# Attention over heads of 64: keys without zero halves, two heads' score products on the two row halves, units in pairs

## The reference, cut to what matters

```python
# first block, per query block
s = jnp.einsum('bqhd,bqjd->bhqj', qb, k_sel).astype(jnp.float32) * scale
p = jax.nn.softmax(jnp.where(valid[:, None], s, neg), axis=-1).astype(v.dtype)
return jnp.einsum('bhqj,bqjd->bqhd', p, v_sel)
```

## Time and profile before

| | us |
|---|---|
| median of 3 runs | 3588.89 (3577.92 to 3591.3) |
| profiled execution, its time | 3573.0 |
| its span, first to last instruction | 3571.1 |
| PE busy | 3265.0 |
| DVE busy | 1950.1 |
| ACT busy | 1306.1 |
| POOL busy | 490.5 |

### The profile page before, as it was taken

How to read it: one execution, slowest core, us unless ns; L and a number is a source line. 1 busy time by engine, 2 the same in 40 slices (tenths; PEclk the granted TensorE clock), 3 DMA queues, 4 the chain that set the end, 5 groups by cost and what they waited for, 6 DMA issues and landing times. The chain is left out here.

```text
span 3571.1 us, 45008 instructions
## 1 busy us (share of the span) xinstructions
PE 3265.0 (91%) x17008; PEld 2733.1 (77%) x17008; DVE 1950.1 (55%) x3638; ACT 1306.1 (37%) x2723; POOL 490.5 (14%) x410
## 2 busy tenths in 40 slices
PE   8998999999989999599979899999798979799996
PEld 6877788878777888488758778888687669688885
DVE  4776434347764343365765456564474864565654
ACT  4454423234544232242542233234342632332324
POOL 1031000010310000003026301010030128001010
PEclk9999999999999999798989999999897989899998
DMA  4111222131112221222000122221321000123231
GB/s 157 62 37 48 85 102 97 48 118 51 48 48 83 95 95 60 90 99 71 1 1 1 36 81 94 98 94 59 110 90 36 1 1 1 57 92 103 88 104 47
DMA packets 37327, 240.04 MB, mean 67 GB/s; under 512 B 4464, under 2 KB 5232, under 8 KB 14960
## 3 DMA queue, kind: packets, MB, share of 16 engines
q1 hardware_dynamic: 36528, 234.96, 19.2%
q10 hardware_dynamic: 576, 2.10, 0.2%
HBM read 234.95 MB, written 2.10 MB: 66 GB/s over the span
## 5 line engine op out<-in xcount | busy, mean ns | idle before, releaser
L259 PE MATMUL ps<-b_hl,bff_whl 128*128 128x512 f32 x704 | 275.4, 391 | 2.8 <-DVE b_hl L618 2.8
L261 PE MATMUL ps<-b_hl,bff_whl 128*128 128x512 f32 x704 | 274.8, 390 | 0.0
L260 PE MATMUL ps<-b_hl,bff_whl 128*128 128x512 f32 x704 | 274.8, 390 | 0.0
L242 DVE SCALAR_TENSOR_TENSOR bff_whl<-ring,b_cols,bff_whl 128x512 fp32r<-128x512 f32 (+1 forms) x224 | 153.2, 745 | 201.7 <-ACT bff_whl L229 201.5
L239 DVE TENSOR_TENSOR aff_whl<-ring,aff_whl 128x512 fp32r<-128x512 f32 x160 | 99.9, 686 | 224.0 <-ACT aff_whl L227 223.9
L259 PE MATMUL ps<-a_hl,aff_whl 128*128 128x512 f32 x512 | 201.3, 393 | 2.8 <-DVE a_hl L618 2.8
L229 ACT ACTIVATE bff_whl<-ring,b_cols 128x512 fp32r<-128x512 f32 (+1 forms) x224 | 136.6, 681 | 180.7 <-PE ps L261 180.7
L259 PE MATMUL ps<-aff_whl,a_u 128*128 128x512 f32 x512 | 202.0, 395 | 0.0
L261 PE MATMUL ps<-aff_whl,a_u 128*128 128x512 f32 x512 | 202.0, 395 | 0.0
L260 PE MATMUL ps<-aff_whl,a_u 128*128 128x512 f32 x512 | 202.0, 395 | 0.0
L260 PE MATMUL ps<-a_hl,aff_whl 128*128 128x512 f32 x512 | 200.9, 392 | 0.0
(11 more groups left out here) (493 smaller groups left out, 8093.2 us busy)
## 6 DMA issues: line engine op xcount, KB each, us to landing
ring<-in_a_w_ff SPq DMA_DIRECT2D x64, 1024.0 KB, 4.7
ring<-in_b_w_up SPq DMA_DIRECT2D x32, 1024.0 KB, 4.9
ring<-in_a_w_in SPq DMA_DIRECT2D x16, 1024.0 KB, 5.4
ring<-in_b_w_down SPq DMA_DIRECT2D x16, 1024.0 KB, 4.8
ring<-in_b_w_in_att SPq DMA_DIRECT2D x12, 1024.0 KB, 4.8
ring<-in_b_w_up SPq DMA_DIRECT2D x16, 768.0 KB, 4.2
ring<-in_b_w_in_conv SPq DMA_DIRECT2D x12, 768.0 KB, 4.4
ring<-in_a_w_out SPq DMA_DIRECT2D x8, 1024.0 KB, 4.9
```

The source lines that it names most:

```text
L242: self.c.nc.vector.scalar_tensor_tensor(out=self.part(j, 1, k), in0=src[:, k, :], scalar=g[:, row + k:row + k + 1], in1=self.part(j, 0, k) ...
L259: nc.tensor.matmul(bank, sh, mh, start=start, stop=False)
L260: nc.tensor.matmul(bank, sh, ml, start=False, stop=False)
L261: return nc.tensor.matmul(bank, sl, mh, start=False, stop=stop)
```

## The change

Keys stand once, with the same values in rows 0 to 63 and 64 to 127, and nothing is cleared. A unit's operands are 64 rows: the rows where its head's queries lie. Units are reordered so that two heads of one query tile follow each other (widths 1, 1, 2, 2, 3, 3, 4, 4), and `softmax_attention` gets an order for them: PE steps by two units, S(i), S(i+1), T(i-4), T(i-3), W(i-6), W(i-5); DVE keeps unit i-7 in step i, ACT copies unit i-4, and p has six buffers. The diff, without the lines that only build lists:

```diff
+        NP = 6 if side_by_side else 3
+        p, pT = sb("p", [P, NP, SEQ]), sb("pT", [P, 2, SEQ])
...
+                def score(i):
+                    qT, kT = units[i][0], units[i][1]
+                    if i >= 4:
+                        pe.wait_ge(probs, i - 3)
+                    nc.tensor.matmul(c.ps[:, i % 4, 0:kT.shape[1]], qT, kT, start=True, stop=True).then_inc(scores, 1)
+
+                def turn(u):
+                    nk = units[u][1].shape[1]
+                    pe.wait_ge(probs, u + 1)
+                    if u >= 2:
+                        pe.wait_ge(probsT, u - 1)
...
+                def weigh(u):
+                    nb = units[u][1].shape[1] // P
+                    pe.wait_ge(probsT, u + 1)
+                    if u >= 2:
+                        pe.wait_ge(kept, u - 1)
...
+                if side_by_side:
+                    for i in range(0, U + 6, 2):
+                        if i >= 4 and i < U:
+                            pe.wait_ge(probs, i - 2)
+                        at(i, score)
+                        at(i + 1, score)
+                        at(i - 4, turn)
+                        at(i - 3, turn)
+                        at(i - 6, weigh)
+                        at(i - 5, weigh)
+                else:
+                    for i in range(U + 4):
+                        at(i, score)
+                        at(i - 2, turn)
+                        at(i - 4, weigh)
...
             def _(dve):
                 step = Steps(dve, step_sem)
-                for i in range(U + 5):
+                lag = 7 if side_by_side else 5
+                for i in range(U + lag):
...
-                    u = i - 5
+                    u = i - lag
...
             def _(act):
-                for i in range(U + 3):
+                lag = 4 if side_by_side else 2
+                for i in range(U + lag + 1):
...
-                        if i >= 3:
-                            act.wait_ge(turned, i - 2)
-                        nc.scalar.activation(p[:, i % 3, 0:nk], c.ps[:, i % 4, 0:nk], ACT.Exp,
+                        if i >= NP:
+                            act.wait_ge(turned, i - NP + 1)
+                        nc.scalar.activation(p[:, i % NP, 0:nk], c.ps[:, i % 4, 0:nk], ACT.Exp,
...
-                    u = i - 2
+                    u = i - lag
...
-                qbT, kbT = sb3("qbT", [P, 2, SEQ]), sb3("kbT", [P, 2, SEQ])
+                qbT, kbT = sb3("qbT", [P, 2, SEQ]), sb3("kbT", [P, SEQ])
...
-                          (kbT[0:HD, 0, :], kbT[HD:P, 1, :]), 1.0)]
-
-                def clear(pool, made):
-                    nc.gpsimd.memset(kbT[HD:P, 0, :], 0.0)
-                    nc.gpsimd.memset(kbT[0:HD, 1, :], 0.0)
+                          kbT[:], 1.0)]
...
+                for pair in range(DSA_H // 2):
                     for t in range(TT):
+                        for h in (2 * pair, 2 * pair + 1):
+                            b = DSA_D * (h % 2)
+                            mask = c.causal if t == 0 else search.tile(t)
+                            units.append((qbT[b:b + DSA_D, pair, t * P:(t + 1) * P],
+                                          kbT[b:b + DSA_D, 0:(t + 1) * P],
...
-            jobs += [(twice(a + g * HD), P, (kT[0:HD, g, 0, :], kT[HD:P, g, 1, :]), 1.0)
+            jobs += [(twice(a + g * HD), P, kT[:, g, :], 1.0)
...
+                for pair in range(NSA_H // 2):
                     for t in range(TT):
+                        for h in (2 * pair, 2 * pair + 1):
+                            g, b = h // NSA_R, HD * (h % 2)
+                            units.append((qT[b:b + HD, pair, t * P:(t + 1) * P], kT[b:b + HD, g, 0:(t + 1) * P],
...
+            softmax_attention(c, "nsa", units, side_by_side=True)
```

More of the change, by code:

```diff
@@ L2230, in rope, with softmax_attention @@
     step(eng.tensor_tensor(x2, x2, t1, ALU.add))
-def softmax_attention(c, name, units, meanwhile=None):
+def softmax_attention(c, name, units, meanwhile=None, side_by_side=False):
     nc = c.nc
@@ L2252, in _ @@
             def _(pe):
[L2253 to L2259, removed]
-                    u = i - 2
-                    if 0 <= u < U:
[L2262 to L2281, removed]
@@ new lines, in score @@
+                def score(i):
[8 more added lines that the diff above has]
+                        pe.wait_ge(probsT, u - 1)
+                    for j in range(nk // P):
+                        ins = nc.tensor.transpose(c.ps[:, 4 + u % 2, j * P:(j + 1) * P],
+                                                  p[:, u % NP, j * P:(j + 1) * P], c.ident)
+                    ins.then_inc(turned, 1)
@@ new lines, in weigh @@
+                def weigh(u):
[3 more added lines that the diff above has]
+                        pe.wait_ge(kept, u - 1)
+                    for j in range(nb):
+                        v = units[u][2](j)
+                        ins = nc.tensor.matmul(c.ps[:, 6 + u % 2, 0:v.shape[1]],
+                                               pT[:, u % 2, j * P:(j + 1) * P], v,
+                                               start=(j == 0), stop=(j == nb - 1))
+                    ins.then_inc(outs, 1)
@@ new lines, in at @@
+                def at(u, do):
+                    if 0 <= u < U:
+                        do(u)
+                if side_by_side:
[13 more added lines that the diff above has]
+                        at(i - 4, weigh)
@@ L3307, in first_block @@
                 units = []
-                for h in range(DSA_H):
+                for pair in range(DSA_H // 2):
                     for t in range(TT):
[L3310 to L3314, removed]
+                        for h in (2 * pair, 2 * pair + 1):
[3 more added lines that the diff above has]
+                                          kbT[b:b + DSA_D, 0:(t + 1) * P],
+                                          lambda j: proj[:, j, A_AV:A_AV + DSA_D], mask,
+                                          mix[:, t, o_b + h * DSA_D:o_b + (h + 1) * DSA_D], None, False))
                 softmax_attention(c, "dsa", units,
                                   lambda pool, step: group_norm(nc, pool, step, out4, heads(A_RG, RET_H, RET_D),
-                                                                mean[:], var[:], half))
+                                                                mean[:], var[:], half), side_by_side=True)
         with ExitStack() as right:
@@ L3430, in attentions @@
                      for a, dst, s in ((B_SQ, sqT, HD ** -0.5), (B_SK, skT, 1.0)) for i in range(SB_H // 2)]
[L3432 to L3436, removed]
+            transpose_tiles(c, "nsaT", jobs)
             out4 = out_n
@@ L3444, in attentions @@
             for i, (kT, v) in enumerate(((ksT, B_VS), (kwT, B_VW))):
-                for h in range(NSA_H):
-                    g = h // NSA_R
+                for pair in range(NSA_H // 2):
                     for t in range(TT):
[L3448 to L3451, removed]
+                        for h in (2 * pair, 2 * pair + 1):
+                            g, b = h // NSA_R, HD * (h % 2)
+                            units.append((qT[b:b + HD, pair, t * P:(t + 1) * P], kT[b:b + HD, g, 0:(t + 1) * P],
+                                          lambda j, v=v, g=g: proj[:, j, v + g * HD:v + (g + 1) * HD], c.causal,
+                                          out4[:, t, h, :], gates[:, t, (i + 1) * NSA_H + h:(i + 1) * NSA_H + h + 1],
+                                          True))
+            softmax_attention(c, "nsa", units, side_by_side=True)
         stick_breaking(c, "stick", sqT, skT, proj[:, :, B_SV:B_SV + SB_H * HD], out_s,
```

6 lines of the change are left out of this document (2 added, 4 removed).

## The result

The changed kernel is 1.3% slower: a median of 3634.78 us (3628.85 to 3647.54, four runs) against 3590.1 for the kernel before on the same chip. The ratio is 1.013, 95% interval [1.0086, 1.0174]. The forecast was 3598 with a range up to 3614, so the time lies outside it. The profiled execution of after is its longest, 3647.54 (span 3645.4), that of before was among the shortest (span 3571.1). The traces are therefore 74.3 apart and the medians about 45.

A forecast was written before the change was run, and what follows sets the result against it. Bound by a loop of VectorE write, weighted sums, next score and mask. NSA +7.8, DSA +2.5 and key tiles -1.2 total +9.1 us: 3582.1 from the profiled execution, 3598 from the 3588.9 median; range 3580 to 3608, reaching 3614.

The forecast's parts named there:

- The loop that binds before: NSA and DSA stages: VectorE write, weighted sums, next score, mask set the pace; 6.34 us per NSA head worked out.
- the array's time is what counts: Rival: given unseen loop slack, both stages fall to VectorE's pace, 5.8 per NSA head; about -20 us, 3569; chance 0.09.
- the chain at 1 to 2 in DSA: Width 1 to 2 step in DSA: last sums 3.39 us after the second width 4 mask, making the step 2.95.
- Halves at once, and their price: Score products: a pair on two row halves costs one product plus 0.28 us for switching, 0.14 on the loop.
- New order: Steady stages in pairs: eight NSA units 13.38 against 12.62 us, +0.76; DSA 13.43 against 12.26, +1.17.
- Fill: Stage start: seven units run ahead of the first keep, not five; gives back 3.0 us per stage.
- Drain: Stage end: last write 9.2 us after the last mask, against 6.17 before; +3.1 us per stage.
- Key tiles: First block: one 128-row key copy replaces two, so retention starts 0.6 us sooner, twice: -1.2 us.
- The clock: Rival: thinner TensorE work drops the stages to 1.2 GHz, 4.4 us per eight units; chance 0.16.
- Its reach: Extent of the low-clock rival: 53 us over all twelve groups; at a third of the time +18, 3616.

The follow-up runs named there:

- a kernel that it was not made for: Kernel before with weighted sums and VectorE's keep one unit later and four buffers for turned probabilities: eight NSA units 13.36 us, ratio 1.0054.
- the filled kernel: Changed kernel plus one unread 128 x 384 product per eight units, ahead of the width 1 sums: ratio 1.0051, NSA 82.6 and 95.7 us.
- the old-order kernel: Changed kernel's 64-row score products and keys, but heads one after the other in the order of the kernel before: eight units 24.37 us, ratio 1.0482.
- its twin: 64-row products in the order before, each from the third unit on issued on both row halves, second result unread: 13.51 us per eight units, ratio 1.0056.
- the padded kernel: Changed kernel's paired unit and engine order, with the zero-padded keys and whole-array products of the kernel before: eight units 12.99 us, ratio 1.0047.
- DVE by pairs: Changed kernel with VectorE masking and reducing two units, then keeping two: eight units 11.88 to 13.38 us, ratio 1.0031; with zero-padded keys 11.88, 1.0002.

## Why the prediction was wrong, by its steps

- **The loop that binds before**: right. It reproduced before, the four steps of after to 0.03 us, and, worked out afterwards, a kernel that it was not made for (13.38 against 13.36). The rival "the array's time is what counts" is out: no kernel came near its 5.8 per head but those whose DVE order was changed (5.94). Two slips in the working change nothing: the chain at 1 to 2 in DSA adds up to 3.35 and not 3.39, and 9.2 less 6.17 is 3.0 and not 3.1.
- **Halves at once, and their price**: right. Four passes in 1.13 us; 0.33 us for eight units on the loop, where the sum had 0.14 on each of the three steps that the loop sets, 0.42. The Trainium skill (TensorE: Matmul & The Clock Gate, "Why this matters for your kernels", small-K row) promises concurrent products on different row groups, and these rows agree.
- **New order**: right while the clock is 1.00 (13.32, forecast 13.38).
- **Fill**: right in kind, 8.59 and 8.33 for the first eight units against 11.0 before, 2.4 to 2.7 given back where 3.0 was taken; in DSA 8.8 against 11.8, 3.0.
- **Drain**: 9.2 forecast from the last mask. In the filled kernel, at 2.4 GHz, it is 9.4 (9.03 from the last reduction, which starts 0.33 after the mask). In after it runs at 1.2 GHz and is 13.2, from 1820.54 to 1833.77:

```profile
1820.54 0.29 DVE L2312 TENSOR_TENSOR ps<-ps,const_b 128x128 f32<-128x128 f32 x1
...
1833.54 0.23 DVE L2326 TENSOR_TENSOR b_mix<-b_mix,nsao 128x64 f32<-128x64 f32 x1
```

- **Key tiles**: right in size, 0.6. From MLA's last write to DSA's first reduction it is 31.28 in layer 1, and it was 31.88. In layer 2 it is 32.93, longer than before. Both lengths occur with either form of the keys, about 1.65 apart: 31.9 and 33.5 where two halves are copied (the latter with four pT in the kernel before), 31.3 and 32.9 where one tile is (two traces have an outlier of 43 to 44 besides). What those 1.65 us are stays open.
- **The clock**: the step that failed. The sum takes every steady group at 1.00, so a fall of the clock stands in it at nothing. It stood among the rivals at 0.16, with a price of 4.4 us per eight units. In the profiled execution 163 of the stages' 272 us are at 1.2 GHz, three fifths, and a group almost wholly at that level takes 19.20, which is 5.9 over 13.32: PE is busy for 46.62 of 48.50 us there, so its transposes, which had slack, count too. What had held the chance down was the busy share: another stage kept 1.00 with 29.66 of 34.00 us busy. The share misled. After was busier at 1.00 (13.45 of 16.90, 80%) than the 77% forecast, and still fell; the old-order kernel was busy all of the time at 1.2 GHz; its twin, just as busy, was at 2.4. Nor can the other stage's products be the difference by their height, since some of them have 64 rows too (L3042).
- **Its reach**: the rival was priced for the twelve groups alone. The drains are at 1.2 GHz too, 3.9 us longer in NSA than at 2.4 (12.9 against 9.0 from the last reduction), which stood in no case. The 6.9 and 5.9 us behind NSA stood in none either, but those the runs don't pin on the change.

What stays open: why the clock falls in after. Its two score products work on both halves at once, as the twins do, so the old-order kernel's low clock is not by itself the explanation; against the padded kernel in the same order after has less for PE to do (80% busy against 90%) and a longer wait at the narrow step (1.16 against 0.45). Which of these counts no run separates. Whole-array products in the same order hold up to the drain; halves in a shorter loop still fall, but less. Why one execution of the same instructions falls in layer 2 and not in layer 1 (the filled kernel) no run explains.

## What to carry to other kernels

Price a change of products by the clock first. Here the halves took work off PE and the stages' clock fell with it (13.32 to 19.20 us for eight units), and with 64-row products one at a time the stage took nearly twice as long (24.37 against 12.62). The busy share of the stage didn't warn of either. When two engines feed each other, write down the loop that closes between them for each step of the pattern; a loop that matches the trace to 0.03 us can tell which reordering helps (DVE by pairs, 11.88) and which only lets other widths meet (13.36), if it is summed anew for each order, which here was done for the second only after the run. A lag moved on both sides of a wait leaves the loop as long as it was and only changes which widths meet.

## What the runs showed of the hardware

- PE busy without a gap can stay at 1.2 GHz: 24.40 of 24.40 us with 64-row score products one at a time (24.37 per eight units). With both row halves at work in the same places it runs at 2.4 GHz (13.51). Other stages with 64-row products one at a time are at 2.4 GHz: retention in the kernel before, at 1.00 from 255 to 280.
- Two products on the two row halves take the time of one (1.13 against 1.08 us for 512 columns), and going to halves and back costs 0.05 to 0.15 us per pair on the steps that the loop sets (2.77, 3.34 and 3.92 against 2.63, 3.29 and 3.77).
- The same instructions can keep 2.4 GHz in one layer and fall to 1.2 four times in the other: 82.6 and 95.7 us for one NSA stage within one execution.
